# Projections of a recurrent mixer in another order, with the decay arithmetic spread over three of them

## The reference

```python
xx = _token_shift(x) - x
xs = x[None] + xx[None] * mix[:, None, None, :]      # six mixtures of x and its left neighbour
r, k, v = jnp.einsum('cbtd,cde->cbte', xs[:3], w_rkv)    # three 1024x1024 projections
xw, xa, xg = xs[3], xs[4], xs[5]
w_raw = (w0 + jnp.tanh(xw @ w1) @ w2).astype(f32)    # three loras: 1024 -> 64/64/160 -> 1024
w_log = -jax.nn.softplus(-w_raw) - 0.5
decay = jnp.exp(-jnp.exp(w_log))
a = jax.nn.sigmoid(a0 + (xa @ a1) @ a2)
g = jax.nn.sigmoid(xg @ g1) @ g2
kk = heads(k * k_k)
kk = kk / jnp.maximum(jnp.sqrt(jnp.sum(kk * kk, axis=-1, keepdims=True)), 1e-12)
k = k * (1.0 + (a - 1.0) * k_a)
r_h, k_h, v_h, a_h = heads(r), heads(k), heads(v), heads(a)
y = _rwkv7_scan(r_h, decay.reshape(B, T, H, N), k_h, v_h, -kk, kk * a_h)
...
y = y + jnp.sum(r_h * k_h * r_k.astype(f32), axis=-1, keepdims=True) * v_h     # the "bonus"
```

## Time and profile before

| | us |
|---|---|
| median of 3 runs | 3325.31 (3321.00 to 3327.82) |
| the profiled execution | 3321.01, its span 3319.2 |
| PE busy in the span | 3146.6 (95%) |
| DVE busy | 2044.8 (62%) |
| ACT busy | 1272.3 (38%) |
| POOL busy | 767.6 (23%) |

### The profile page before, as it was taken

How to read it: one execution, slowest core, us unless ns; L and a number is a source line. 1 busy time by engine, 2 the same in 40 slices (tenths; PEclk the granted TensorE clock), 3 DMA queues, 4 the chain that set the end, 5 groups by cost and what they waited for, 6 DMA issues and landing times.

```text
span 3319.2 us, 42623 instructions
## 1 busy us (share of the span) xinstructions
PE 3146.6 (95%) x16753; PEld 2701.4 (81%) x16753; DVE 2044.8 (62%) x3717; ACT 1272.3 (38%) x2159; POOL 767.6 (23%) x495
## 2 busy tenths in 40 slices
PE   7878999989999999999998999999999997999998
PEld 6456989878888887888887678999999996887777
DVE  5386565564333355333367655988878765887878
ACT  4364443433322334322235332335444453333332
POOL 0000010100000020000000300576776752353543
PEclk9888999999999999999998799999999998999999
DMA  3131121233333332333232012478878888999997
GB/s 120 34 84 65 58 71 52 64 108 89 95 96 100 115 95 89 95 96 99 85 91 66 1 49 92 152 253 293 292 277 325 269 307 299 359 349 349 340 346 266
DMA packets 229351, 538.17 MB, mean 162 GB/s; under 512 B 22352, under 2 KB 88144, under 8 KB 227616
## 3 DMA queue, kind: packets, MB, share of 16 engines
q1 hardware_dynamic: 191712, 399.09, 36.7%
q0 software_dynamic: 37440, 136.36, 11.2%
HBM read 482.92 MB, written 52.46 MB: 161 GB/s over the span
## 4 chain that ended last, share of the span: by engine, by line
PE 67%; DVE 14%; DMA 10%; POOL 4%; ACT 3%; issue 2%; SPq 1%; DVEq 0%; ACTq 0%; POOLq 0%
PE bank L344 23%; PE bank L347 14%; PE bank L2205 9%; DMA gl<-acts 6%; PE bank L2633 4%; POOL etl L2193 3%; DMA eu<-in_peer_u 3%; PE bank L975 2%; DVE vsl L2677 2%; PE bank L985 2%; PE bank L2362 2%; DVE y_row L2250 2%; PE bank L1780 2%; PE bank L939 1%; PE bank L927 1%
## 5 line engine op out<-in xcount | busy, mean ns | idle before, releaser
L294 DVE TENSOR_TENSOR wl<-raw,wh 128x1024 fp32r<-128x1024 f32 (+3 forms) x239 | 293.8, 1232 | 644.9 <-ACT wh L279 644.8
L279 ACT CAST wh<-raw 128x1024 fp32r<-128x1024 f32 (+3 forms) x239 | 247.4, 1037 | 646.2 <-PE bank L344 358.7
L2193 POOL TENSOR_TENSOR etl<-eu,eth 128x1024 fp32r<-128x1024 f32 x128 | 319.5, 2497 | 433.9 <-ACT eth L2189 432.3
L2205 PE MATMUL bank<-peerhh,eth 128*128 128x384 f32 x1024 | 349.6, 341 | 28.3 <-POOL etl L2193 26.6
L2205 PE MATMUL bank<-peerhl,eth 128*128 128x384 f32 x1024 | 343.5, 335 | 0.0
L2205 PE MATMUL bank<-peerhh,etl 128*128 128x384 f32 x1024 | 343.5, 335 | 0.0
L2633 PE MATMUL bank<-vsh,coefh 128*128 128x512 f32 x768 | 302.8, 394 | 19.2 <-DVE coefl L2688 19.0
L2633 PE MATMUL bank<-vsh,coefl 128*128 128x512 f32 x768 | 301.7, 393 | 0.0
L2633 PE MATMUL bank<-vsl,coefh 128*128 128x512 f32 x768 | 301.5, 393 | 0.0
L2230 POOL DMA_INDIRECT taken<-in_peer_v,gb x128 | 218.7, 1708 | 300.1 <-DVE y_row L2250 271.4
L2189 ACT CAST eth<-eu 128x1024 fp32r<-128x1024 f32 x128 | 135.5, 1059 | 237.7 <-DMA eu<-in_peer_u 233.9
(11 more groups left out here) (542 smaller groups left out, 7320.1 us busy)
## 6 DMA issues: line engine op xcount, KB each, us to landing
eu<-in_peer_u SPq DMA_DIRECT2D x128, 512.0 KB
vb<-in_peer_v SPq DMA_DIRECT2D x128, 512.0 KB
raw<-in_ada_w SPq DMA_DIRECT2D x48, 512.0 KB, 3.9
acts<-eg SPq DMA_DIRECT2D x128, 192.0 KB
coefs<-stage SPq DMA_DIRECT2D x12, 2048.0 KB, 8.5
gd<-coefs SPq DMA_DIRECT2D x16, 1536.0 KB, 14.6
gl<-acts SPq DMA_DIRECT2D x128, 192.0 KB
raw<-in_ffn_w_gate SPq DMA_DIRECT2D x44, 512.0 KB, 3.6
```

What stands on the lines that cost most here:

```text
L279: act.copy(parts_of(c)[0], raw_of(c)).then_inc(*up("w rounded", c))
L294: dve.tensor_tensor(lo, raw_of(c), hi.bitcast(F32), ALU.subtract).then_inc(*up("w split", c))
L2193: pool.tensor_tensor(Et[j % 3][1], Eu[j % 2], Et[j % 3][0].bitcast(F32), ALU.subtract).then_inc(*up("u split", j))
L2205: t = pe.matmul(b, tb[un][:, k * 128:(k + 1) * 128], peer_h[hn][:, k, 1:4, :], start=k == 0 and i == 0, stop=k == 7 and i == 2)
```

## The change

The plans are put in another order, both in the weight stream and in `PROJ_ORDER`: w1, a1, g1, k, r, v. With that the loras' results (the log decay `lw` and `a`) are there when k is projected, and the decays are cut in four parts:

- `dve_sums`: scans and tiny operations, beside k, in place in `lw`;
- the squares of the keys beside k and r; their eight sums on PE in two blocks of four after r's first two pieces; root and inverse after r's third;
- `act_factor` and `dve_keyed` (norms and factor): tiles 0 to 3 beside r's last pieces, tiles 4 to 7 beside v's first four;
- `act_exps` and `dve_decays` (bonus product and exponentials) beside v, with two sets of temporaries `pts`, used in turn.

The bonus sums share one bank, copied once. The splits of two further pieces leave the opening loop.

```diff
-    st.plan("k", W[1], D, 0, D)
-    st.plan("r", W[0], D, 0, D)
     for n in "wa":
...
     st.plan("g1", I["rwkv_g1"][0], D, 0, 160)
-    st.plan("v", W[2], D, 0, D)
+    for n, w in (("k", 1), ("r", 0), ("v", 2)):
+        st.plan(n, W[w], D, 0, D)
...
-    rkt = [f("rk", 128, 512), f("rk", 130, 512)]
-    pt_ = [f("pt", 132, 512), f("pt", 134, 512), f("pt", 136, 512)]
+    rkt = [gb1[:, 0:512], gb1[:, 512:1024]]
+    pts = [[f("pt", kb + 2 * i, 512) for i in range(3)] for kb in (132, 16)]
+    squared = [pts[0][0], pts[0][2], *rkt]
+    factors = [*mt, *rkt, *mt, *mt]
...
-    PROJ_ORDER = [1, 0, 3, 4, 5, 2]
+    PROJ_ORDER = [3, 4, 5, 1, 0, 2]
...
+    def pe_bonus(pe, on_pe, k):
+        if k == 0:
+            bonus_bank[:] = banks.take(("bonus",), ("bonus",))
+        b, before = bonus_bank
+        for what in before:
+            on_pe.wait_ge(*at(*what))
+        on_pe.wait_ge(*at("decays dve", k, "rk"))
...
+    def act_factor(act, on_act, k):
         on_act.wait_ge(*at("aa", k))
         on_act.wait_ge(*at("dve step", "1-ka"))
...
+        if k >= 4:
+            on_act.wait_ge(*at("decays dve", k - 2, "keyed"))
+        act.activation(factors[k], aa[:, k, :], ACT.Identity, scale=vec("ka", k),
+                       bias=small[:, 200 + k:201 + k]).then_inc(*up("decays act", k, "factor"))
+
+    def act_exps(act, on_act, k):
+        on_act.wait_ge(*at("decays dve", k, "shifted"))
         if k >= 2:
+            on_act.wait_ge(*at("decays dve", k - 2, "all"))
...
+        pt = pts[k % 2]
         for ch in range(4):
             cs = slice(ch * 128, (ch + 1) * 128)
-            t = act.activation(pt_[0][:, cs], pt_[1][:, cs], ACT.Exp, scale=-E_HALF, bias=svp[:, k, ch:ch + 1])
+            t = act.activation(pt[0][:, cs], lw[:, k, cs], ACT.Exp, scale=-E_HALF, bias=svp[:, k, ch:ch + 1])
...
+    def dve_keyed(dve, on_dve, k):
         on_dve.wait_ge(*at("norms in"))
+        on_dve.wait_ge(*at(*copied("k", k)))
         dve.scalar_tensor_tensor(ta[:, k, :], k_[:, k, :], vec("kk", k), ta[:, k, :], ALU.mult,
...
         on_dve.wait_ge(*at("decays act", k, "factor"))
-        dve.tensor_tensor(k_[:, k, :], k_[:, k, :], rk, ALU.mult).then_inc(*did("k"))
...
+        dve.tensor_tensor(k_[:, k, :], k_[:, k, :], factors[k], ALU.mult).then_inc(*up("decays dve", k, "keyed"))
...
+    def pe_beside(pe, on_pe, plan, n):
+        if plan == "r" and n < 2:
+            for k in range(4 * n, 4 * n + 4):
+                pe_keys(pe, on_pe, k)
+        if plan == "v" and n:
+            pe_bonus(pe, on_pe, n - 1)
+
+    def act_beside(act, on_act, plan, n):
+        if plan == "k" and n >= 4:
+            act_keys(act, on_act, n - 4)
+        if plan == "r" and n == 0:
+            for k in range(4, KD):
+                act_keys(act, on_act, k)
+        if plan == "r" and n == 2:
+            act_key_norms(act, on_act)
+        if plan == "r" and n == 5:
+            for k in range(4):
+                act_factor(act, on_act, k)
+        if plan == "v":
+            for k in ((4, 5), (), (6,), (7,))[n] if n < 4 else ():
+                act_factor(act, on_act, k)
+            act_exps(act, on_act, n)
+
+    def dve_beside(dve, on_dve, plan, n):
+        if plan == "k":
+            dve_sums(dve, on_dve, n)
+        if plan == "r" and n == 2:
+            dve_keys(dve, on_dve)
+        if plan == "r" and n >= 6:
+            for k in (2 * n - 12, 2 * n - 11):
+                dve_keyed(dve, on_dve, k)
+        if plan == "v":
+            if n < 4:
+                dve_keyed(dve, on_dve, 4 + n)
+            dve_decays(dve, on_dve, n)
...
             if ft:
                 act_mix(act, on_act, PROJ_ORDER[0], ft - 1)
-            if ft in (2, 4):
-                cast(1 + ft // 2)
...
             if k:
                 dve_mix_rest(dve, on_dve, PROJ_ORDER[0], k - 1)
-            if k in (2, 4):
-                rest(1 + k // 2)
```

More of the change, by code:

```diff
@@ L570, in xs_of, with pe_keys, act_keys, act_key_norms @@
         return xs[0][:, k, :], xs[1][:, k, :]
-    def pe_keys(pe, on_pe, n):
-        k = n - 1
+    def pe_keys(pe, on_pe, k):
         if k == 0:
             key_bank[:] = banks.take(("keys",), ("act root", "keys"))
[L576 to L579, removed]
             on_pe.wait_ge(*at("tables in", "heads"))
[L581 to L594, removed]
+        b, before = key_bank
+        for what in before:
+            on_pe.wait_ge(*at(*what))
+        on_pe.wait_ge(*at("keys square", k))
+        pe.matmul(b[0:16, :], heads[:, 14 - 2 * k:30 - 2 * k], squared[k % 4], start=k == 0,
+                  stop=k == KD - 1).then_inc(*up("bank full", "keys", k))
+    def act_keys(act, on_act, k):
+        on_act.wait_ge(*at(*copied("k", k)))
+        if k >= 4:
+            on_act.wait_ge(*at("bank full", "keys", k - 4))
+        act.activation(squared[k % 4], k_[:, k, :], ACT.Square, scale=vec("kk", k)).then_inc(*up("keys square", k))
+    def act_key_norms(act, on_act):
+        on_act.wait_ge(*at("bank full", "keys", KD - 1))
+        act.sqrt(norms, banks["keys",][0:16, :]).then_inc(*up("act root", "keys"))
     def dve_keys(dve, on_dve):
@@ L610, in pool_keys @@
                                *up("norms in", by=16))
[L612 to L622, removed]
@@ L624, in act_decays @@
-    def act_decays(act, on_act, k):
-        if k >= KD:
-            return
+    def pe_bonus(pe, on_pe, k):
+        if k == 0:
+            bonus_bank[:] = banks.take(("bonus",), ("bonus",))
+        b, before = bonus_bank
+        for what in before:
+            on_pe.wait_ge(*at(*what))
+        on_pe.wait_ge(*at("decays dve", k, "rk"))
+        for tt in range(NT):
+            t = pe.matmul(b[:, tt * 16 + 2 * k:tt * 16 + 2 * k + 2], rkt[k % 2][:, tt * 128:(tt + 1) * 128],
+                          bones[:, 0:128:64], start=True, stop=True)
+        t.then_inc(*up("bank full", "bonus", k))
@@ L651, in act_decays, with dve_sums @@
         t.then_inc(*up("decays act", k, 1))
-        on_act.wait_ge(*at("decays dve", k, "shifted"))
         act.activation(se[:, k, :], se[:, k, :], ACT.Exp, scale=-E_HALF).then_inc(*up("decays act", k, 3))
[L655 to L674, removed]
+    def dve_sums(dve, on_dve, k):
```

110 lines of the change are left out of this document (55 added, 55 removed).

## The result

| | before | after |
|---|---|---|
| median, same chip, 5 runs each | 3326.91 (3321.00 to 3331.20) | 3298.84 (3291.24 to 3304.73) |
| the profiled execution, its span | 3321.01, 3319.2 | 3298.84, 3297.1 |
| mean granted clock over the span | 0.973 | 0.973 |

The ratio is 0.9917, interval 0.9898 to 0.9936: 21 to 34 us saved. Two later comparisons of the same kernel gave 0.9918 and 0.9923. The forecast was 3302, 23.5 us less.

The account below looks back on a forecast made before the run. Bound: a chain of waits, PE in k and r, mixing in the loras, DVE in v. The new steps, summed, end g2 at 264.5 for 287.99; 3325.3 - 23.5 = 3301.8, so 3302 us, range 3291 to 3317.

Parts of the forecast that it names:

- The opening: Opening loop without two weight splits of 1.13 us each: last rest ends at 35.1, w2 starts at 37.2 us.
- The sums beside k, the squares, the root, the inverse: Beside k and r: sums of 1.7 us per piece and squares hidden; inverse done 25 us after r's start.
- The norms: Beside r: norm reads land 44 us after r's start, DVE asks at 45; no wait, margin one us.
- PE leads: In v: PE's step of 6.4 us exceeds DVE's 6.2 then 4.3 and ACT's 5.6 or 4.8; v takes 55.1.
- the second wait: At v's second bonus sum: operand ready at 21.0 us, PE due at 19.4, so 1.6 us lost.
- The 0.7 us for a bank: In v: the second group's last bank must be copied out by ACT behind the fourth step's exponentials, costing 0.7 us.
- three engines might wait for one another: Rival in v: mutual waits add up to 1.5 us a step, 12 us given back, 3314; chance 0.18.
- What made v long before: Old v, 79.3 us: DVE set the pace at 8.12 us a step, where PE needed 5.67 or 5.68.
- w2's clock: Before k: w2 was taken to run at half clock for all its 14.0 us, as in the old kernel.
- the first rival: w2 at full clock, 7.1 us as a2 takes: 6.9 us more gained, 3295; chance 0.18.
- Nothing lost after g2: After g2: scan constants and scan start from g2's end and move with it, keeping the 23.5 us.
- the range's lower end: Whole kernel: 3291 us, from w2 at full clock and v at its lower bound of 52.8.

Follow-up runs that it names:

- e4: Changed kernel with maximum and inverse of the key norms two pieces of r later on DVE: 0.9957 of the old kernel, 3306.93 us.
- e2: Changed kernel without the spreading: sums, factor and products of all eight tiles back in v's steps; 0.9976 of the old kernel, 3315.35 us.
- e1_again: Second run of the changed kernel with one set of temporaries for the exponentials: 0.9935 of the old kernel, 3302.13 us; the first run gave 0.9942, 3304.55.
- e6: Changed kernel with six tiles of r's mixture formed beside k's last three pieces: 0.9903 of the old kernel, 3295.38 us.
- e7: Changed kernel with both the roundings between w2's and a2's sigmoids and r's mixture beside k: 0.9866 of the old kernel, 3276.69 us.
- a0_after: The changed kernel run again without edit: 0.9918 of the old kernel, 3295.66 us.
- a1_after: The changed kernel run once more without edit, in another comparison: 0.9923 of the old kernel, 3297.49 us.
- e5: Changed kernel with ACT rounding the next lora's mixture tile by tile between the sigmoids of w2 and a2: 0.9895 of the old kernel, 3288.77 us.

## Why the prediction was right, and where it was not

By its own steps, forecast and profiled execution:

| step | forecast | measured |
|---|---|---|
| last rest of the opening loop ends | 35.1 | 35.05 |
| w2 starts | 37.2 | 37.87 |
| w2 | 14.0 | 14.00 |
| k's first matmul | 89.8 | 90.48 |
| k ends | 135.0 | 134.97 |
| gap, r's start | 2.9, 137.9 | 2.87, 137.84 |
| r ends | 191.6 | 192.05 |
| gap, v's start | 4.0, 195.6 | 4.03, 196.08 |
| v | 55.1 | 54.61 |
| g2, its end | 13.8, 264.5 | 13.58, 264.27 |

The rows behind the points that the table doesn't settle:

*The opening.* DVE's two slots went as forecast. DVE's last rest, w1's last matmul, and ACT's rows at the tanh:

```profile
33.59 1.46 DVE L837 TENSOR_TENSOR mixedl<-mix,mixedh 128x512 fp32r<-128x512 f32 x2
```

```profile
36.52 0.63 PE L343 MATMUL bank<-mixedh,wl 128*64 128x512 f32 x1
```

```profile
34.34 1.28 ACT L799 ACT_TABLE_LOAD   x1
37.18 0.59 ACT L799 ACTIVATE gb<-bank 64x512 f32<-64x512 f32 x1 [1.56 <-PE bank L343]
```

The table load lay ahead of the wait for PE and cost nothing. w2 was 0.7 us late because w1 was: its last matmul began at 36.52 us and took 0.63. The forecast let three matmuls follow the last rest; six ran back to back at half clock (34.33 to 37.15), so PE and not DVE set w1's end.

- *The sums beside k, the squares, the root, the inverse*: nothing of them shows on the path; k went through in one chain.
- *The norms.* The place and the kind of the wait were right (e4). The margin was 2.7 for 1 us: the second read landed in 13.8 us for the 15.7 of the earlier trace rows, it was issued 0.9 us later, counted from r's start, and DVE came 0.7 us later. The margin depends on how long the read takes: in e4 the same read took 16.5.
- *v.* PE leads, as forecast, behind a start that DVE sets. To the end of the second wait it took 20.74 us (216.82 less 196.08) for 21.0; inside, the first two pieces were slower by a us and the wait 0.37 for 1.6. In ten profiled executions, all but e2's and the old kernel's, this stretch took 20.7 us, while PE's wait at its end lay between 0.34 and 0.96 us: what PE loses at half clock there comes off its wait. The 0.7 us for a bank didn't come; with one set, in e1_again, it did, as 1.14. That three engines might wait for one another is refuted by the rows of DVE, which doesn't wait from 213.01 to 247.67 us.
- *What made v long before.* e2 bears out the reading of the earlier trace rows: with sums and products back in the step it is 8.1 us, and about 19 us of the gain are gone.
- *w2's clock* is the step that failed as it was put. "I keep it" took half clock for a trait of the kernel. Ten profiled executions have the same instructions of TensorE up to w2: it took 14.0 us in four (the changed kernel's first, the repeat of e1, e6, e7) and 7.1 in six. Its reason doesn't hold either: PE was to be less busy before w2 than before the change, but at its lower clock it was busy for 10.38 of 13 us with fewer matmuls (21), where the old kernel had 8.25 of 13 with 28, both before a w2 at 0.50; in a0_after it was 9.41 of 13, before a w2 at 1.00. So the first rival's event came true in six of these ten executions, but not its 6.9 us: in a0_after v and g2 gave back 1.6 and 5.0, in a1_after 1.6 and 3.3, and g2's end lies within 1.4 us of the other. That the forecast's end of g2 held there too is luck: nothing in the forecast provides for a clock that falls in v and g2.
- *Nothing lost after g2.* The span kept 22.1 of 23.7 us. Executions of one kernel differ by more than that difference after g2: 3032.8 us from its end in the first profile, 3038.3 in a0_after, with a mean clock of 0.973 and 0.970.
- *Two sums.* Three pieces and one bonus sum make 19.2 us and not 19.4, and by its own terms the range's lower end is 3292.6 and not 3291; neither decides anything.
- The forecast took 23.5 us off the old median; by the medians of its comparison it was 28, with an interval that holds both.

## What to carry to other kernels

Where two engines hand each other the pieces of a step, take out of the step what doesn't depend on it and put it beside a stage in which that engine is idle: here moving the sums to k and half of the products to r was worth about twice the rest of the change, while the new order and doubled buffers without it left the step at 8.1 us. Before a stage's time goes into a forecast, look at its clock in several executions: w2 took 14.0 or 7.1 us with the same instructions. When a moved transfer becomes a wait near the path, forecast its margin and test it by moving it once more. Look for what an engine does in bulk ahead of what others wait for: taking turns tile by tile between the sigmoids and the next rounding put k 9 us earlier (a first long chain at 82.85 for 91.83, both behind a w2 of 14 us).

## What the runs showed of the hardware

TensorE's granted clock differs from execution to execution of one program. In the changed kernel's first execution it stayed at 0.50 (1.2 GHz) through all of w2, which kept PE busy for 13.99 of 14.00 us; in a0_after it was 1.00 (2.4 GHz) in the same place. In g2 of a0_after it fell from 1.00 to 0.50 between two of the rows above, while PE ran plain fp32 matmuls back to back. The Trainium skill (TensorE: Matmul & The Clock Gate, Part 1: The HAM clock gate (the "warmup" mystery)) says that the gate isn't timed by the kernel's start, so that the point of change varies from run to run. That w2 took 14.0 us in one execution and 7.1 in another agrees in so far as it varies. By its rule that activity releases the throttle neither w2's 14 us at 0.50 nor the fall inside g2 would be expected, and these rows speak against it for such matmuls. They don't give a rule in its place: the same matmuls kept 1.00 in a0_after's w2 and in the first execution's g2 (13.60 of 13.60 us busy), and w2's clock doesn't tell g2's (14.0 us with 13.58 in the first profile and e7_both, 14.0 with 16.93 in e1_again, 7.1 with 13.58 in e4 and e5). What sets the clock stays open.
